# Two edits in a two-block transformer kernel: the last modulation pieces loaded ahead of the query weights, and the second block's output projection in full precision

## The chip, the cores and the metric

The kernel runs on one core of a Trainium2 chip. The metric is the device time of one execution in microseconds (us). Before the change the median of three runs is 1758.28 us (1758.21 to 1758.53).

## The reference

The input is a sequence of 256 tokens of width 1024 (two token blocks of 128) in float32. It goes through two different transformer blocks, each with two layers. What matters here, shortened:

```
# first block, per layer
shift, scale, gate, ... = split(silu(c) @ w_ada + b_ada)     # modulation, 6 x 1024 values
h = rmsnorm(x) * (1 + scale) + shift
q_lat, kv_lat, k_pe, sb_qkv, mb_qkv, gates = split(h @ w_in)
q  = rmsnorm(q_lat) @ w_uq ;  kv = rmsnorm(kv_lat) @ w_ukv   # latent attention (MLA)
merged = g_a*(o_mla @ w_o_mla) + g_b*(o_sb @ w_o_sb) + g_c*(o_mb @ w_o_moba)
x = x + gate * (merged @ w_out) ; then a squared-ReLU feed-forward

# second block, per layer
proj = rms_norm(x) @ w_in
mix = concat(o_fox, o_nsa, o_dil)                            # 256 + 512 + 256 columns
x = x + rms_norm(mix @ w_out)                                # the output projection
x = x + rms_norm(conv_ffn(rms_norm(x), w_up, conv, w_down))
```

## The kernel before

**Weights and the ring.** All weights stream from memory in pieces of at most 128 x 1024 float32 values (512 KB) through a ring of ten slots (`ring`, RAW = 10). The list `stream` is the order of the pieces, made at lines 424 to 488. SyncE issues the loads in that order (`load`, line 582): the load of piece u waits until piece u-10, which had the same slot, has been used by its reader. SyncE is one queue, so a load that waits holds all behind it. TensorE tells that a piece is free by an increment that rides on the next matmul it issues (the list `owed`); for the modulation pieces VectorE is the reader and tells it itself (`ada_used`, line 1919).

**Two kinds of product.** Most linear layers are split: a weight piece is rounded by ScalarE into a `high` part (line 1372, buffers `high` of four, or a spare place in another tensor), VectorE subtracts that from the raw piece into a `low` part (line 1813), the features are likewise held as two parts (`featT_r` and `featL`), and `three` (line 798) makes three products in the reduced format float32r: high x high, high x low, low x high. In the profile these are the matmuls on `high`, `gates_r`, `big_r` or `ring_r` with `featT_r` or `oT_r`. Other layers are plain (`plain`, `linear`, `linear_pair`): one product in full float32 from the raw piece in the ring, with no copy and no subtraction. In the profile a full-precision matmul leaves two records. `split` pieces pass through ScalarE (`highs(n)`) and VectorE (`split_unit`, `first_quarters(n)`: a unit is four pieces, a quarter is one) at places written out by hand in each engine's program.

**First block, layer 0, around the change.** The projection w_in is computed in eleven units (u = 0 to 10), then the query weights w_uq (two units of three pieces), then w_ukv (two pieces), then modulation tile 9, then the gate columns unit by unit as filling between the attention heads. The modulation product silu(c) @ w_ada is made by VectorE, piece by piece: `ada_step` (line 1906) multiplies the two halves of a piece by a scalar per partition and adds them up in `ada`, four steps for 512 columns; TensorE then sums over the partitions. The last four of these steps before MLA are done between the two copies of q out of the banks (line 2197), in layer 0 alone: in layer 1 there are none at this place (`0 if l else 4`). The gate unit's pieces stand in the stream between w_uq and those four modulation pieces. Gate unit 3 follows behind w_ukv; its copies are `highs(2 if i in (2, 3) else 0)` inside ScalarE's MLA loop (line 1599), ahead of that turn's exponentials, and its subtractions stand at the same turns on VectorE (line 2216), ahead of that turn's score subtraction.

**Second block, around the change.** The attention loop (`softmax_heads`) leaves eight chunks of 128 features x 256 tokens in an output bank each. VectorE copies six of them to `oT`; two turns later ScalarE rounds such a chunk into `featT_r` (line 1469) and VectorE takes the rest into `featL` (line 2031). The last two chunks VectorE rounds and subtracts itself, straight from the bank (lines 2039, 2040). The output projection is `two_as_ready` (line 855): tiles (token block t, column half u) in the order (0,0), (0,1), (1,0), (1,1), each over 8 chunks with `three`, and inside the last tile, after its first piece, the transposes of token block 0 for the next layer (`flip_tile`). Pieces are told free while token block 1 is computed. Behind it ScalarE squares the banks, GpSimd makes the reciprocal root (`rstd_parts`), VectorE applies it (`products`, `normed`, `scale_tokens`), the transposes follow, ScalarE and VectorE turn them into feature parts (`features_out`), and w_up starts (`two_by_tiles`, then `channels`). Between these steps the pieces of the output weights and of w_up are rounded and subtracted.

Of the kernel before, what the change touches and what calls it, by code (L numbers as in the profile page):

```python
# [8 lines left out]
F32 = mybir.dt.float32  # L9
F32R = mybir.dt.float32r  # L10
I32 = mybir.dt.int32
ACT = mybir.ActivationFunctionType
# [101 lines left out]
def two_blocks(nc, x_in, c_in, positions, w_ada, b_ada, norm1_g, norm2_g, w_in, q_norm_g, w_uq,  # L114
# [5 lines left out]
    with ctx:  # L120
# [79 lines left out]
        spare_out_2 = slots(gates_r, 0, PIECE) + slots(big_r, 6 * PIECE, 7 * PIECE)  # L200
        assert T * N_IN <= 6 * PIECE
# [81 lines left out]
        out_high, out_low = sem("out_high"), sem("out_low")  # L283
# [111 lines left out]
        def split_given(*pieces, spare=None):  # L395

            split_units.append(pieces)
            low_units.append(pieces)
            for j, it in enumerate(pieces):
                put(it, spare[j] if spare else None, False, 12)  # L400

# [22 lines left out]
        for l in range(LAYERS1):  # L424
# [8 lines left out]
            for u in range(11):  # L433
                c0 = u * ATT_W if u < 9 else ATT + 512 * (u - 9)
                split(w_in[l], (c0, min(c0 + ATT_W, ATT) if u < 9 else c0 + 512), beside=IN_STEPS[l][u - 1] if u else 0,
                      spare=spare_1 if u == 0 else None)
            for u in range(2):
                plain(*[cols_piece(w_uq[l], k0, k0 + 2, (UQ_W * u, UQ_W * u + UQ_W)) for k0 in range(0, QR // P, 2)])
            gate_unit = split(w_in[l], (ATT + 2 * 512, ATT + 3 * 512), later=True)
            for _ in range(0 if l else 4):  # L440
                ada_piece()
# [24 lines left out]
        for l in range(LAYERS2):  # L466
# [4 lines left out]
            for u in range(2):  # L471
# [6 lines left out]
                split_given(cols_piece(w, 0, 2, (cols.start, cols.stop), split=True),  # L478
                            *[piece(2, 512, [(slice(0, HD), all_k, all_n, lower[:, j:j + 2, :]),
                                             (slice(HD, P), all_k, all_n, upper[:, j:j + 2, :])], split=True) for j in (0, 2)],  # L480
                            cols_piece(w, 6, 8, (cols.start, cols.stop), split=True), spare=spare_out_2 if u else None)
# [243 lines left out]
        def _(pe):  # L725
# [514 lines left out]
            for l in range(LAYERS2):  # L1240
# [97 lines left out]
        def _(act):  # L1338
# [110 lines left out]
            def softmax_heads(jobs, beside=None, out0=None):  # L1449
                for i in range(len(jobs) + 2):  # L1450
# [14 lines left out]
                    if out0 is not None and i >= 5 and jobs[i - 5]["last"]:  # L1465
                        out0 += 1
                        act.wait_ge(outputs.read, out0)
                        c = jobs[i - 5]["chunk"]
                        act.activation(featT_r[:, c, :], oT[:, c, :], ACT.Copy).then_inc(out_high, 1)
# [181 lines left out]
            for l in range(LAYERS2):  # L1651
# [19 lines left out]
                highs(2)  # L1671
# [34 lines left out]
                softmax_heads(second_jobs, compressed, attention_out[l] - KD)  # L1706
# [878 lines left out]
```

## Time and profile before

| | |
|---|---|
| median of the runs | 1758.28 us |
| profiled execution | 1757.0 us |
| its span | 1755.3 us |
| TensorE (PE) busy | 1687.2 us, 96% |
| VectorE (DVE) busy | 1180.3 us, 67% |
| ScalarE (ACT) busy | 858.0 us, 49% |
| GpSimd (POOL) busy | 146.7 us, 8% |
| chain that ended last | TensorE 70%, VectorE 15%, ScalarE 5%, loads 4% |

The profile is of one execution. The span is the time from the first to the last recorded instruction. A line such as L1372 is a line of the kernel; a helper's line stands for all that it issues, so the matmuls all have L741 (`mm`) and the transposes L750 (`flip`), and one goes by the names of the tiles. Brackets at the end of a timeline's row give the idle time of the engine just before and what ended it. The granted clock is a share of 2.4 GHz: 1.00 is the upper level, 0.50 the lower one (1.2 GHz), values between are a mixture. `PEld` is the load of the stationary operand, which overlaps the matmuls.

### The profile page before, as it was taken

To read this page: it belongs to the slowest core of one execution; us is meant where nothing else is said; L and a number is where in the kernel's file an instruction comes from. 1 tells how busy PE (TensorE), PEld (TensorE's weight loads), DVE (VectorE), ACT (ScalarE), POOL (GpSimd) and SP (SyncE) were. 2 spreads that over 40 slices of the span, in tenths; PEclk is the share of its full clock that TensorE was granted. 3 is DMA by queue.
4 is the path that set the end of the run, shared out by engine and by line. 5 is a ranking of instruction groups with operands and counts; after the bars stand their busy time and mean duration, and the time that the engine had idled before them with its cause. 6 is when DMAs were issued, how large, how long until landed. Compare 5 with 4: busy or idle time off the path is not lost.

```text
span 1755.3 us, 24848 instructions
## 1 busy us (share of the span) xinstructions
PE 1687.2 (96%) x9315; PEld 1389.8 (79%) x9315; DVE 1180.3 (67%) x2033; ACT 858.0 (49%) x1505; POOL 146.7 (8%) x296
## 2 busy tenths in 40 slices
PE   6999799999999999999999999989999999999998
PEld 3897576589987896774799878767998787679986
DVE  5676455866766885556835675757788767667885
ACT  3354264256443442652455344475555544755552
POOL 1210011000000000220000000041000000410000
PEclk8999999999999999999999999989999999999999
DMA  9886424557863986326456656703665467046552
GB/s 341 296 280 223 149 61 141 189 192 260 291 203 122 365 272 198 116 76 217 144 204 202 193 163 201 203 2 122 214 183 187 157 219 193 1 135 210 184 181 84
DMA packets 185912, 323.71 MB, mean 184 GB/s; under 512 B 13540, under 2 KB 101184, under 8 KB 185792
## 3 DMA queue, kind: packets, MB, share of 16 engines
q1 hardware_dynamic: 183200, 320.54, 56.4%
q10 hardware_dynamic: 2592, 1.57, 0.3%
q8 instruction: 74, 1.21, 0.3%
q14 instruction: 46, 0.38, 0.1%
HBM read 321.02 MB, written 1.05 MB: 183 GB/s over the span
## 4 chain that ended last, share of the span: by engine, by line
PE 70%; DVE 15%; ACT 5%; DMA 4%; issue 3%; POOL 2%; SPq 0%; DVEq 0%; POOLq 0%; ACTq 0%
PE bank L741 67%; DVE ring_r L1813 6%; PE bank L750 3%; ACT sm L1458 1%; DMA ring<-in_w_in 1%; DVE ada L1918 1%; DMA ring<-in_w_ada 1%; POOL sm L667 1%; ACT high L1372 1%; DMA ring<-in_w_ff 1%; DVE gates_r L1838 1%; DVE sm L1998 1%; DVE gates L2496 0%; DVE oT_r L1845 0%; DVE gates L2494 0%
## 5 line engine op out<-in xcount | busy, mean ns | idle before, releaser
L1813 DVE TENSOR_TENSOR ring_r<-ring,high 128x1024 fp32r<-128x1024 f32 (+3 forms) x390 | 460.5, 1197 | 271.1 <-ACT high L1372 262.7
L1372 ACT ACTIVATE high<-ring 128x1024 fp32r<-128x1024 f32 (+3 forms) x390 | 402.1, 1037 | 482.1 <-PE bank L741 357.1
L741 PE MATMUL bank<-ring_r,featT_r 128*128 128x512 f32 (+3 forms) x928 | 355.5, 383 | 0.0
L741 PE MATMUL bank<-high,featT_r 128*128 128x512 f32 (+3 forms) x712 | 277.2, 389 | 8.9 <-DVE oT_r L1845 2.8
L741 PE MATMUL bank<-featT_r,high 128*128 128x256 f32 x960 | 272.6, 284 | 0.1
L741 PE MATMUL bank<-featT_r,ring_r 128*128 128x256 f32 x960 | 271.6, 283 | 0.0
L741 PE MATMUL bank<-oT_r,high 128*128 128x256 f32 x960 | 271.6, 283 | 0.0
L741 PE MATMUL bank<-high,oT_r 128*128 128x512 f32 (+3 forms) x712 | 270.6, 380 | 0.0
L741 PE MATMUL bank<-high,gates_r 128*128 128x512 f32 x736 | 230.2, 391 | 3.6 <-DVE ring_r L1813 2.6
L741 PEld LDWEIGHTS bank<-ring_r,featT_r 128*128 128x128 f32 x928 | 175.8, 189 | 27.2 <-issue 0.5
L741 PEld LDWEIGHTS bank<-featT_r,high 128*128 128x128 f32 x960 | 184.2, 192 | 1.2 <-DVE ring_r L1813 0.9
L741 PEld LDWEIGHTS bank<-oT_r,high 128*128 128x128 f32 x960 | 184.3, 192 | 0.3 <-issue 0.2
L741 PEld LDWEIGHTS bank<-featT_r,ring_r 128*128 128x128 f32 x960 | 184.2, 192 | 0.0
L741 PE MATMUL bank<-ring_r,gates_r 128*128 128x512 f32 x432 | 168.2, 389 | 0.0
L741 PEld LDWEIGHTS bank<-high,featT_r 128*128 128x128 f32 x712 | 133.9, 188 | 40.9 <-issue 11.8
L741 PEld LDWEIGHTS bank<-high,gates_r 128*128 128x128 f32 x736 | 138.2, 188 | 34.9 <-DVE ring_r L1813 4.6
L741 PEld LDWEIGHTS bank<-high,oT_r 128*128 128x128 f32 x712 | 133.9, 188 | 21.3
L1918 DVE SCALAR_TENSOR_TENSOR ada<-ring,tiny,ada 128x512 f32<-128x512 f32 x154 | 115.5, 750 | 12.7 <-DMA ring<-in_w_ada 7.8
L667 POOL TENSOR_TENSOR sm<-sm,rs 128x128 f32<-128x128 f32 (+1 forms) x160 | 77.2, 514 | 463.9 <-DVE rs L2021 441.0
L1458 ACT ACTIVATE sm<-sm,mx 128x128 f32<-128x128 f32 (+1 forms) x160 | 71.5, 447 | 47.5 <-DVEq L2004 47.3
L741 PEld LDWEIGHTS bank<-ring_r,gates_r 128*128 128x128 f32 x432 | 81.1, 188 | 16.3
L656 POOL TENSOR_SCALAR stat<-stat 128x1 f32<-128x1 f32 x26 | 13.3, 510 | 828.0 <-ACT sm L1390 827.9
(267 smaller groups left out, 2205.3 us busy)
## 6 DMA issues: line engine op xcount, KB each, us to landing
ring<-in_w_ff SPq DMA_DIRECT2D x128, 512.0 KB, 5.0
ring<-in_w_ada SPq DMA_DIRECT2D x96, 512.0 KB, 5.7
ring<-in_w_up SPq DMA_DIRECT2D x176, 256.0 KB, 3.4
ring<-in_w_in SPq DMA_DIRECT2D x64, 464.0 KB, 5.3
ring<-in_w_in SPq DMA_DIRECT2D x48, 512.0 KB, 5.5
ring<-in_w_in SPq DMA_DIRECT2D x48, 474.0 KB, 5.0
ring<-in_w_down SPq DMA_DIRECT2D x44, 512.0 KB, 3.5
ring<-in_w_out SPq DMA_DIRECT2D x24, 512.0 KB, 5.3
```

The costliest lines, as they stand in the source:

```text
L656: pool.tensor_scalar(stat[:, 4 + t:5 + t], stat[:, 2 * t:2 * t + 1], EPS, None, ALU.add).then_inc(pool_chain, 1)
L667: ins = pool.tensor_tensor(sm[:, n, a:z], sm[:, n, a:z], rs[:, n, t:t + 1].to_broadcast([P, z - a]), ALU.mult)
L741: ins = pe.matmul(o, a, b, start=start, stop=stop, skip_group_check=True)
L750: ins = pe.transpose(o, a, ident[0:n, 0:n])
L1372: act.activation(it["high"], it["raw"], ACT.Copy).then_inc(high_ready, 1)
L1458: ins = act.activation(sm[:, n, cols], sm[:, n, cols], ACT.Exp, scale=-1.0, bias=mx[:, n, t:t + 1], accum_out=rs[:, n, t:t + 1])
L1813: dve.tensor_tensor(it["low"], it["raw"], it["high"].bitcast(F32), ALU.subtract).then_inc(low_ready, 1)
L1838: dve.tensor_tensor(low_, src, high_.bitcast(F32), ALU.subtract).then_inc(hid_split, 1)
L1918: link(dve.scalar_tensor_tensor(out=acc, in0=row, scalar=by, in1=acc, op0=ALU.mult, op1=ALU.add))
L1998: ins = dve.tensor_tensor_reduce(out=sm[:, n, a:z], in0=b[:, a:z], in1=cst[:, j["mask"] + a:j["mask"] + z], scale=-j["scale"], scalar=3e38 ...
```

## The change

In the first block, layer 0, the four modulation pieces move ahead of the w_uq pieces in the stream (four DMAs in SyncE's queue, ahead of six of w_uq and four of the gate unit), and the four steps on VectorE move ahead of the gate unit's four subtractions, the copies of k_pe and the first copy of q. TensorE's order is the same.

In the second block, both layers, the eight pieces of the output weights become plain: no copies by ScalarE (8 per layer), no subtractions by VectorE (8 per layer). The chunks stay in `oT` in full precision; the roundings and subtractions of the chunks go, and all eight are copied from the bank once. The projection is `linear_pair`: the same order of tiles and the same transposes inside the last tile, after its first piece, with 32 full-precision products where there were 96 reduced ones. The pieces of w_up keep their places on ScalarE and VectorE relative to the steps of the norm, but for one: VectorE now has two quarters ahead of the transposes' features and none behind them, where it had three and one. The places of `high` and the count back to the piece that was there before follow from the shorter list.

```diff
-        spare_out_2 = slots(gates_r, 0, PIECE) + slots(big_r, 6 * PIECE, 7 * PIECE)
...
+            for _ in range(0 if l else 4):
+                ada_piece()
             for u in range(2):
                 plain(*[cols_piece(w_uq[l], k0, k0 + 2, (UQ_W * u, UQ_W * u + UQ_W)) for k0 in range(0, QR // P, 2)])
             gate_unit = split(w_in[l], (ATT + 2 * 512, ATT + 3 * 512), later=True)
-            for _ in range(0 if l else 4):
-                ada_piece()
             for u in range(2):
                 plain(cols_piece(w_ukv[l], 0, KVR // P, (512 * u, 512 * u + 512)))
...
-                split_given(cols_piece(w, 0, 2, (cols.start, cols.stop), split=True),
-                            *[piece(2, 512, [(slice(0, HD), all_k, all_n, lower[:, j:j + 2, :]),
-                                             (slice(HD, P), all_k, all_n, upper[:, j:j + 2, :])], split=True) for j in (0, 2)],
-                            cols_piece(w, 6, 8, (cols.start, cols.stop), split=True), spare=spare_out_2 if u else None)
+                plain(cols_piece(w, 0, 2, (cols.start, cols.stop)),
+                      *[piece(2, 512, [(slice(0, HD), all_k, all_n, lower[:, j:j + 2, :]),
+                                       (slice(HD, P), all_k, all_n, upper[:, j:j + 2, :])]) for j in (0, 2)],
+                      cols_piece(w, 6, 8, (cols.start, cols.stop)))
...
# TensorE, second block
-                seen.more(out_low, KD - 2)
                 deep_tile0.append((made[id(for_dve)], made[id(outputs)]))
-                two_as_ready({(1, 1, 1): (scaled, 0)}, (for_dve, for_dve, outputs, outputs))
+                linear_pair(lambda c, t: oT[:, c, t * P:(t + 1) * P], scaled, (1, 1))
...
# ScalarE, second block
                 turns_out(nsa_turns + fox_turns)
-                highs(2)
...
-                softmax_heads(second_jobs, compressed, attention_out[l] - KD)
-                highs(6)
+                softmax_heads(second_jobs, compressed)
+                highs(2)
                 square_banks(deep_tile0[LAYERS1 + 2 * l], (0, 0), (0, 1))
-                highs(2)
                 square_parts((0, 0), (0, 1))
...
# VectorE, attention loop: the last two chunks had been rounded and subtracted from the bank
+                        b = tile(outputs)
+                        read(outputs, dve.tensor_copy(out_view(jobs[i - 4]["chunk"], fill is not None),
+                                                      b[:, 0:S].rearrange("p (t s) -> p t s", t=T)))
...
# VectorE, first block
                 modulation_out(l, IN_OUT[l][10])
+                for _ in range(0 if l else 4):
+                    ada_step()
                 split_unit()
...
                     read(for_dve, dve.tensor_copy(qmla[:, 1, u * UQ_W:(u + 1) * UQ_W], b[:, 0:UQ_W]))
-                    for _ in range(4 if u == 0 and l == 0 else 0):
-                        ada_step()
...
# VectorE, second block
-                first_quarters(2)
                 turns_out(key_turns + dil_turns)
...
                 first_quarters(2)
-                split_unit()
                 seen.more(bc_loaded, 32)
                 products(0, 0)
                 normed(0)
                 scale_tokens([0])
-                first_quarters(3)
+                first_quarters(2)
                 features_out(pcol[:, 2 + l, 96:104], None, True, [0])
-                first_quarters(1)
                 products(0, 1)
```

## Rows read from the trace of the kernel before

**Rows 1.** The page's first part: TensorE's busy time, share, instructions.
```profile
PE 1687.2 (96%) x9315; PEld 1389.8 (79%) x9315; DVE 1180.3 (67%) x2033; ACT 858.0 (49%) x1505; POOL 146.7 (8%) x296
```
**Rows 2.** Windows: stretch, its us, TensorE busy (count), granted clock, DMA share, GB/s.
```profile
159.54:192.74 33.20, 29.01 (x93) 0.95 0.50 169
192.74:231.64 38.90, 33.54 (x197) 0.91 0.40 136
675.44:702.01 26.57, 26.17 (x85) 1.00 0.63 211
702.01:734.14 32.13, 30.87 (x197) 1.00 0.32 99
...
1184.43:1208.38 23.95, 23.20 (x104) 1.00 0.40 129
```
**Rows 3.** Windows of TensorE inside these stages, and of full-precision products (the last).
```profile
160.35:176.07 15.72, 15.72 (x50) 1.00 0.73 248
...
180.07:188.71 8.64, 8.64 (x16) 0.80 0.18 63
...
215.93:222.08 6.15, 6.15 (x22) 0.52 0.73 271
291.86:312.56 20.70, 20.70 (x48) 1.00 0.56 183
```
**Rows 4.** The chain that ended last, layer 0: start, us, what.
```profile
175.46 4.47 DMA ring<-in_w_ukv
...
204.83 5.53 DMA ring<-in_w_in
```
**Rows 5.** Timeline of SyncE's loads, layer 0 of the first block.
```profile
155.87 1.73 SPq L589 DMA_DIRECT2D ring<-in_w_uq  x2
...
175.46 6.27 SPq L589 DMA_DIRECT2D ring<-in_w_ukv  x2
...
203.47 8.75 SPq L589 DMA_DIRECT2D ring<-in_w_in  x10
```
**Rows 6.** Timeline of VectorE, the same stage.
```profile
160.92 0.16 DVE L1940 SCALAR_TENSOR_TENSOR mod<-mod,pcol 128x4 f32<-128x4 f32 x1 [0.15 <-DVE mod L1936]
...
172.64 3.22 DVE L1918 SCALAR_TENSOR_TENSOR ada<-ring,tiny,ada 128x512 f32<-128x512 f32 x4 [1.13 <-DMA ring<-in_w_ada]
```
**Rows 7.** DMA issues between 152 and 157.3: count, size, median us to landing.
```profile
ring<-in_w_uq SPq DMA_DIRECT2D x2, 384.0 KB, 3.6
```
**Rows 8.** Timeline of TensorE, projection and first w_up units, second block's layer 0.
```profile
1184.43 0.50 PE L741 MATMUL bank<-high,featT_r 128*128 128x512 f32 x1 [0.99 <-DVE oT_r L2040]
...
1185.69 0.39 PE L741 MATMUL bank<-high,oT_r 128*128 128x512 f32 x1
...
1202.04 0.39 PE L741 MATMUL bank<-gates_r,oT_r 128*128 128x512 f32 x1
1202.66 1.09 PE L750 MATMUL bank<-cst,wide 128*128 128x128 f32 x8 [0.23 <-DVE wide L1806]
...
1208.38 0.47 PE L741 MATMUL bank<-high,featT_r 128*128 128x512 f32 x1 [0.52 <-DVE oT_r L1845]
...
1221.39 0.47 PE L741 MATMUL bank<-high,featT_r 128*128 128x512 f32 x1 [0.44 <-DVE oT_r L1845]
```
**Rows 9.** VectorE, last chunk of the attention, second block's layer 1.
```profile
1532.80 0.42 DVE L2039 CAST featT_r<-bank 128x256 fp32r<-128x256 f32 x1 [1.46 <-PE bank L741]
1533.25 0.42 DVE L2040 TENSOR_TENSOR oT_r<-bank,featT_r 128x256 fp32r<-128x256 f32 x1
```
**Rows 10.** ScalarE's copies of w_up pieces, projection, second block's layer 1.
```profile
1547.89 1.06 ACT L1372 ACTIVATE high<-ring 128x1024 fp32r<-128x1024 f32 x1 [0.30 <-PE bank L741]
...
1552.63 1.06 ACT L1372 ACTIVATE high<-ring 128x1024 fp32r<-128x1024 f32 x1 [1.26 <-DMA ring<-in_w_up]
```
**Rows 11.** ScalarE at the GELU, second block's layer 0.
```profile
1127.45 0.76 ACT L1675 ACTIVATE gates<-bank 30x256 f32<-30x256 f32 x2 [2.42 <-PE bank L741]
```
**Rows 12.** The waits, whole span: us in total, times, longest.
```profile
PE bank L750 <- POOL sm L667: 12.0, 16, 5.4
```

More of the change, by code:

```diff
@@ L199, in two_blocks @@
         spare_2 = slots(gates_r, 0, PIECE) + slots(sm_r, PIECE) + slots(pT_r, 0)
-        spare_out_2 = slots(gates_r, 0, PIECE) + slots(big_r, 6 * PIECE, 7 * PIECE)
-        assert T * N_IN <= 6 * PIECE
         spare_gates = slots(oT_r, 8 * S) + slots(kvm_r, PIECE) + slots(gates_r, 5 * PIECE) + [None]
@@ L282, in two_blocks @@
         evac_act = sem("evac_act")
-        out_high, out_low = sem("out_high"), sem("out_low")
         ready_dve = sem("ready_dve")
@@ L393, in split @@
             return pieces
[L395 to L400, printed above, removed]
         def split_together():
@@ L1447, in turns_out, with softmax_heads @@
                     read(ins)
-            def softmax_heads(jobs, beside=None, out0=None):
+            def softmax_heads(jobs, beside=None):
                 for i in range(len(jobs) + 2):
@@ L1464, in softmax_heads @@
                             copy_out(pT[:, (2 * (i - 2) + e) % NPT, :], b[:, 0:3 * P])
[L1465 to L1469, printed above, removed]
             def stick_heads(l, beside):
@@ L1985, in gates_out, with out_view @@
                 read(outputs, dve.tensor_copy(n, b[:, :]))
+            def out_view(c, l1):
+                return out_of(c) if l1 else oT[:, c, :].rearrange("p (t s) -> p t s", t=T)
             def softmax_heads(jobs, beside=None, fill=None):
@@ L2027, in softmax_heads @@
                         gates_out()
-                    if fill is None and 6 <= i < len(jobs) + 3 and jobs[i - 6]["last"]:
-                        c = jobs[i - 6]["chunk"]
-                        seen.more(out_high)
-                        dve.tensor_tensor(featL[:, c, :], oT[:, c, :], featT_r[:, c, :].bitcast(F32), ALU.subtract).then_inc(out_low, 1)
                     if i >= 4 and jobs[i - 4]["last"]:
-                        b, c = tile(outputs), jobs[i - 4]["chunk"]
-                        if fill is not None:
-                            read(outputs, dve.tensor_copy(out_of(c), b[:, 0:S].rearrange("p (t s) -> p t s", t=T)))
-                        elif i < len(jobs) + 1:
-                            read(outputs, dve.tensor_copy(oT[:, c, :], b[:, 0:S]))
-                        else:
-                            link(dve.tensor_copy(featT_r[:, c, :], b[:, 0:S]))
-                            read(outputs, dve.tensor_tensor(featL[:, c, :], b[:, 0:S], featT_r[:, c, :].bitcast(F32), ALU.subtract))
+                        b = tile(outputs)
+                        read(outputs, dve.tensor_copy(out_view(jobs[i - 4]["chunk"], fill is not None),
+                                                      b[:, 0:S].rearrange("p (t s) -> p t s", t=T)))
             def stick_heads(beside, fill):
```

## The prediction

> **What bounds the kernel now.** I read the busy shares first. TensorE works for 1687.2 of 1755.3 us [rows 1], so nothing that another engine gains counts unless TensorE waits for it, and every microsecond that TensorE is given counts in full. TensorE is idle for only 68 us. The question is therefore which of its idle time the first edit takes away, and how much work the second edit adds.
>
> Next I compared the two layers of the first block over the same stages [rows 2]. They issue the same work, except that layer 0 has one more modulation tile and four more modulation pieces in the stream of loads. From the start of the query weights to the first transposes of MLA, layer 0 takes 33.20 us and layer 1 takes 26.57. From there to the next turn (the stick-breaking heads) it is 38.90 against 32.13. The granted clock is 0.95 and 0.91 in layer 0 and 1.00 in layer 1. The chain of waits names what stands in layer 0 and not in layer 1: a load of w_ukv of 4.47 us and a load of w_in of 5.53 us [rows 4]. Both have one reason, the ring of ten slots. Before the change the stream is 6 pieces of w_uq, 4 gate pieces, 4 modulation pieces, 2 of w_ukv, then the pieces of gate unit 3. So w_ukv takes the slots of the last two w_uq pieces, and unit 3 takes those of the gate pieces just ahead of it. SyncE issues w_ukv only at 175.46, the second 5.9 us later because the last w_uq piece is told free by the first matmul that itself waits for w_ukv; unit 3 is issued from 203.47 on [rows 5].
>
> **Edit 1, the four modulation pieces ahead of w_uq.** The numbers N+... count pieces from the first w_uq of before. After: modulation N to N+3, w_uq N+4 to N+9, gate N+10 to N+13, w_ukv N+14 and N+15, unit 3 N+16 to N+19. A piece waits for the one ten before it. So w_ukv waits for the first two w_uq pieces, and unit 3 for the last four. From w_uq on, these distances are those of layer 1, whose windows are thus a measured picture of what is left.
> - Stage A: 33.20 - 26.57 = 6.63, less the extra modulation tile of layer 0 (0.81 us, from 159.54 [rows 2] to w_uq's start at 160.35 [rows 3]): 5.8 us. It is made of the wait of 4.0 us between the end of w_uq (176.07) and the start of w_ukv (180.07), and of w_ukv's eight products (16 records), which take 8.64 us at a granted clock of 0.80 [rows 3], the 1.2 GHz level for a part of them after the idle time, where eight at 0.8625 (below) would take 6.9.
> - Stage B: 38.90 - 32.13 = 6.8 us. ScalarE stands in its queue at a copy that waits for unit 3's load, with the exponentials of the next head pair behind it, and TensorE waits for these through VectorE and GpSimd. Then 6.15 us run at a clock of 0.52, the lower level [rows 3].
>
> What the moved step costs. On VectorE the four steps now stand ahead of the gate unit's four subtractions and the first copy of q. Two steps take 3.22 us and the links between them [rows 6], so four take about 6.4: from 161.1 (end of the modulation sum) to 167.5. The gate loads wait for them one by one, at 162.6, 164.2, 165.9 and 167.5, where they went at 157.65 before. With 4 to 4.4 us to land, ScalarE's last copy ends at 173 and VectorE's last subtraction at 174.3, the q copies at 175.7 and 176.7. TensorE wants that unit only after w_ukv, at 183.9, so the cover is 9 us. w_ukv stands behind the gates in SyncE's queue: issued at about 168, landed at 173, wanted at 176.1. The cover is 3 us; beyond it each microsecond costs one, and then the clock. w_uq is the tight one: its first piece now takes a slot that is told free at 155.87 [rows 5], lands 3.6 us later [rows 7], at 159.5, and TensorE wants it at 160.35; the second and third have 0.6 to 1 us. I take nothing for it. Bounds of edit 1: 12.6 us at best (5.8 + 6.8), 8.9 at worst, if w_uq comes 2 us late and the clock falls for it (2 + 1.7, the latter what w_ukv lost). I take 12.6.
>
> **Edit 2, the output projection.** Before, 96 products per layer of 128x512 in the reduced format. 72 starts lie between 1185.69 and 1202.04 [rows 8]: 0.2271 us each, 21.8 us. After, 32 full-precision products of the same shape. Such a product is in the trace in the first block: 48 records, two to a product, so 24 products in 20.70 us [rows 3], 0.8625 each, 27.6 us. That is 5.8 us more per layer, 11.6 for both. It stands on TensorE and nothing hides it.
>
> The row has a full-precision product at 0.8625 / 0.2271 = 3.8 times a reduced one. The Trainium skill (FP8 and Floating Point Precision, section TensorE Precision Notes) has it as four passes through the array. By that rule, as an estimate, a product would take 4 x 0.2271 = 0.908 us and the sum would be 2.9 us longer; I go by the row.
>
> What comes back, per layer:
> - The last chunk is copied once from its bank, where before it was rounded and then subtracted, 0.42 us each [rows 9]. TensorE starts the projection 0.42 us sooner.
> - In the projection TensorE waits 0.23 us for the scaled tokens and 0.52 for their parts [rows 8]. Both tiles of token block 0 are now full 13.8 us after the start instead of 10.9, the scaled tokens follow 7.3 us behind (from 1184.43 + 10.9 to the flip's 1202.66), at 21.1, and the flip now stands at 22.4, so the 0.23 goes. The parts: w_up pieces 2 and 3 take slots that come free 16.7 and 18.4 us after the start. They land 3.8 to 4.7 us later (before: released at about 1547.9, copied at 1552.63 [rows 10]), so ScalarE copies the second from 23.1 to 24.2, squares and splits features until 26.5, VectorE, which subtracts that piece first, until about 28.2, and TensorE is done at 28.6. The 0.52 goes, with a slack of only 0.4 us.
> - VectorE has no quarter ahead of the products of token block 1 now, so that chain is 1.1 us shorter; TensorE reaches it 0.5 us sooner. The 0.44 us wait in the first w_up units [rows 8] goes: 0.4.
> Sum: 0.42 + 0.75 + 0.4 = 1.6 per layer, bounds 0.4 (only the copy) and 2.5 (the slack also takes time off other waits).
>
> ScalarE loses 16 copies of 1.06 us (as in [rows 10]) and 12 small ones, VectorE 16 subtractions of whole pieces and 16 small ones. I price them at nothing: where two copies stood before the GELU, ScalarE then waits 2.42 us for TensorE [rows 11]. At most they cut into the 12.0 us in which TensorE waits for GpSimd's rescaling [rows 12], 5.35 of which are stage B's; GpSimd is paced by itself there. Loads, their sizes and number stay.
>
> **The sum**, against the profiled execution's own 1757.0 us (span 1755.3 and 1.7 around it): -12.6 + 11.6 - 3.2 = -4.2, thus 1752.8. The median of the runs shown, 1758.28, is 1.3 us over the profiled execution, and what I predict is the median: 1754.1 us. Less than 0.2% (3.5 us) either way can't be told from no change.
>
> **Rivals.**
> 1. Unit 3 is still late: its copy needs not only the load but a free high buffer, released by the gate unit. Then only stage A is gained, -5.8 + 8.4 = +2.6: 1760.9, slower. Against it: layer 1 has the same buffers and waits 0.9 us. It decides if more than 4.2 us of stage B stay. 6%.
> 2. The full-precision products run slower in their new place. At a granted clock of 0.80 w_ukv's take 1.08 us [rows 3]; at that price 64 of them add 14 us: 1768, clearly slower. It decides from 0.93 us each. For it: the attention ahead has many short waits. Against it: the clock is 1.00 there [rows 2]. 5%.
> 3. The w_up pieces in the projection are late, the ring being held longer: 1 to 2 us of wait in each layer, 1757. The thin slack speaks for it, the relief on VectorE and ScalarE against. 13%.
> 4. w_uq late: 3.7 us are lost in edit 1, 1757.8. 8%.
> 5. A full-precision product takes four times the pitch of a reduced one here: 64 x 0.046 = 2.9 us more, 1757.0. The 24 products speak against it. 4%. (The skill's page named above would have it so.)
> 6. The relief does reach TensorE: 2 to 4 us more, 1751. GpSimd's pace speaks against. 8%.
> The forecast has 56%, its own range is 1752.5 to 1756.
>
> **How the numbers follow.** Faster by over 0.2% means under 1754.8: most of the forecast's share (48 of 56) and rival 6: 56%. Within: the rest of it and rivals 3 to 5 and most of 1 (up to 1761.8): 37%. Slower: rival 2 and a tail of 1: 7%. The range of 1750.8 to 1758.6 leaves out rivals 1 and 2 and tails.
>
> **What would show it.** In layer 0 the windows of the two stages shrink to 27.4 and 32.1 us with a clock of 1.00, and no wait of TensorE for w_ukv or of ScalarE for w_in of over 1 us is left there. w_uq's first product starts at 160.35, not later. The projection shows 64 records per layer at 0.43 us, 28.7 us from its start to w_up's instead of 23.9, with no wait of over 0.2 us at its end. The rest shifts as a block. I am wrong if layer 0 stays longer than layer 1 by more than the modulation tile, or if a full-precision product takes over 0.9 us.

## The result and the profile after

The changed kernel takes 1749.18 us (median of four runs, 1745.93 to 1749.50) against 1758.40 for the kernel before (1758.21 to 1758.82): ratio 0.9943, 95% interval 0.9926 to 0.9960, or -9.2 us by the medians where -4.2 was forecast (the ratio is one of mean times; by it the difference is -10.0). Its profiled execution took 1749.38 us (span 1747.6). The direction was right; the time lies 1.6 us below the range of 1750.8 to 1758.6. First the page's busy times after, which answer to [rows 1]:

```profile
PE 1695.3 (97%) x9251; PEld 1380.8 (79%) x9251; DVE 1156.3 (66%) x2001; ACT 838.3 (48%) x1477; POOL 142.5 (8%) x296
```

TensorE works 8.1 us more and the span is 7.7 us shorter, so its idle time fell from 68 to 52 us. Of these 16 us the forecast had accounted for about 11 (7.9 in stages A and B, by the difference of span and busy time in [rows 2], and 3.2 in edit 2).

The windows after, of TensorE alone (stretch, its us, busy time and count, granted clock, DMA share, GB/s): stages A and B of layer 0, the run of query and w_ukv products, the projection to w_up's first product, and twice the stretch from the start of the projection to the second unit of w_up.

```profile
160.24:187.61 27.37, 27.16 (x93) 1.00 0.77 262
187.61:219.53 31.92, 30.90 (x196) 1.00 0.31 100
161.05:183.58 22.53, 22.53 (x66) 1.00 0.90 307
1171.17:1199.22 28.05, 28.05 (x73) 1.00 0.33 100
1171.17:1211.51 40.34, 40.34 (x128) 1.00 0.34 105
1523.09:1563.43 40.34, 40.34 (x128) 1.00 0.33 105
```

And the last stretch before the change, which no row ahead of the prediction shows, layer 0 and layer 1 of the second block:

```profile
1184.43:1221.39 36.96, 35.71 (x161) 1.00 0.36 114
1533.73:1570.67 36.94, 35.75 (x161) 1.00 0.37 115
```

Against [rows 2], stage A went from 33.20 to 27.37 and stage B from 38.90 to 31.92, with the clock at 1.00. The query weights and w_ukv now run without a gap (22.53 us busy of 22.53). The last-named stretch, from the projection's first product to the first product of w_up's second unit, I call P from here on. It grew by 3.38 and 3.40 us. This is the number to explain: by my terms it should have grown by 5.8 - 0.75 - 0.4 = 4.65.

TensorE after, around the projection of layer 0, to compare with [rows 8] (the helper lines have moved: matmuls are now L731, transposes L740):

```profile
1171.17 22.58 PE L731 MATMUL bank<-ring,oT 128*128 128x512 f32 x52 [0.53 <-DVE oT L2016]
1193.59 1.04 PE L740 MATMUL bank<-cst,wide 128*128 128x128 f32 x8
1194.47 5.32 PE L731 MATMUL bank<-ring,oT 128*128 128x512 f32 x12
1199.22 0.80 PE L731 MATMUL bank<-high,featT_r 128*128 128x512 f32 x1
...
1207.83 1.04 PE L740 MATMUL bank<-cst,wide 128*128 128x128 f32 x8
1208.62 0.48 PE L731 MATMUL bank<-gates_r,featT_r 128*128 128x512 f32 x1
...
1211.51 0.47 PE L731 MATMUL bank<-high,featT_r 128*128 128x512 f32 x1
```

I call each group of eight transposes of scaled tokens a turn: the first is that of token block 0, the second that of block 1. The length of a turn is the time from its first transpose to the product behind it. The 52 records before the first turn are 26 products in 22.42 us, 0.862 each, as forecast. Not one wait is left in P behind its start. The second turn takes 0.79 us (1207.83 to 1208.62); before the change it took 1.13:

```profile
1216.81 1.09 PE L750 MATMUL bank<-cst,wide 128*128 128x128 f32 x8
1217.94 0.50 PE L741 MATMUL bank<-gates_r,featT_r 128*128 128x512 f32 x1
```

### The profile page after: what moved, and what is told of

The parts are those of the page before. It is cut to its first block, busy times and chain, and to the rows that moved or that the text cites. A ratio compares the mean times of both kernels' runs of the same rounds, so it can differ in the third digit from the quotient of the medians.

```text
span 1747.6 us, 24642 instructions
## 1 busy us (share of the span) xinstructions
PE 1695.3 (97%) x9251; PEld 1380.8 (79%) x9251; DVE 1156.3 (66%) x2001; ACT 838.3 (48%) x1477; POOL 142.5 (8%) x296
## 4 chain that ended last, share of the span: by engine, by line
PE 74%; DVE 14%; ACT 5%; DMA 3%; issue 2%; POOL 2%; DVEq 0%; SPq 0%; POOLq 0%; ACTq 0%
PE bank L731 71%; DVE ring_r L1795 5%; PE bank L740 3%; ACT sm L1447 2%; DMA ring<-in_w_in 1%; POOL sm L657 1%; DVE ada L1900 1%; ACT high L1361 1%; DVE gates_r L1820 1%; DVE sm L1984 1%; DMA ring<-in_w_ff 1%; DMA ring<-in_w_ada 0%; DVE gates L2470 0%; DVE gates L2468 0%; DVE gates_r L1819 0%
## 5 line engine op out<-in xcount | busy, mean ns | idle before, releaser
L1795 DVE TENSOR_TENSOR ring_r<-ring,high 128x1024 fp32r<-128x1024 f32 (+3 forms) x382 | 451.3, 1197 | 274.8 <-ACT high L1361 267.4
L1361 ACT ACTIVATE high<-ring 128x1024 fp32r<-128x1024 f32 (+3 forms) x382 | 393.5, 1037 | 484.5 <-PE bank L731 347.7
L731 PE MATMUL bank<-ring_r,featT_r 128*128 128x512 f32 (+3 forms) x864 | 330.5, 383 | 0.0
L731 PE MATMUL bank<-featT_r,high 128*128 128x256 f32 x960 | 273.0, 284 | 0.0
L731 PE MATMUL bank<-featT_r,ring_r 128*128 128x256 f32 x960 | 271.8, 283 | 0.0
L731 PE MATMUL bank<-oT_r,high 128*128 128x256 f32 x960 | 271.7, 283 | 0.0
L731 PE MATMUL bank<-high,featT_r 128*128 128x512 f32 (+3 forms) x680 | 264.7, 389 | 4.9 <-DVE ring_r L1795 2.6
L731 PE MATMUL bank<-high,oT_r 128*128 128x512 f32 (+3 forms) x680 | 257.9, 379 | 0.0
L731 PE MATMUL bank<-high,gates_r 128*128 128x512 f32 x736 | 230.1, 390 | 3.4 <-DVE ring_r L1795 2.6
L731 PEld LDWEIGHTS bank<-featT_r,high 128*128 128x128 f32 x960 | 184.3, 192 | 0.6 <-DVE ring_r L1795 0.3
L731 PEld LDWEIGHTS bank<-oT_r,high 128*128 128x128 f32 x960 | 184.4, 192 | 0.5 <-issue 0.4
L731 PEld LDWEIGHTS bank<-featT_r,ring_r 128*128 128x128 f32 x960 | 184.4, 192 | 0.0
L731 PEld LDWEIGHTS bank<-ring_r,featT_r 128*128 128x128 f32 x864 | 163.9, 190 | 25.3 <-issue 1.0
L731 PE MATMUL bank<-ring_r,gates_r 128*128 128x512 f32 x432 | 168.2, 389 | 0.0
L731 PEld LDWEIGHTS bank<-high,gates_r 128*128 128x128 f32 x736 | 138.2, 188 | 34.4 <-DVE ring_r L1795 4.3
L731 PEld LDWEIGHTS bank<-high,featT_r 128*128 128x128 f32 x680 | 127.6, 188 | 34.4 <-issue 9.2
L731 PEld LDWEIGHTS bank<-high,oT_r 128*128 128x128 f32 x680 | 127.7, 188 | 19.9
L731 PEld LDWEIGHTS bank<-ring_r,gates_r 128*128 128x128 f32 x432 | 81.2, 188 | 16.2
```

What stands on the lines that cost most here:

```text
L731: ins = pe.matmul(o, a, b, start=start, stop=stop, skip_group_check=True)
L1361: act.activation(it["high"], it["raw"], ACT.Copy).then_inc(high_ready, 1)
L1795: dve.tensor_tensor(it["low"], it["raw"], it["high"].bitcast(F32), ALU.subtract).then_inc(low_ready, 1)
```

## The experiments

All times are medians; a ratio is that to the kernel before, run on the same chip, and a difference in us stated behind a ratio is the ratio's. The whole time of one kernel scatters: the kernel before took 1753.0 to 1761.4 us over its 36 runs here. P does not: in the seven traces with the full-precision projection (five) or with extra products instead (two) it is 40.34 to 40.38, both layers.

### Edit 1 alone

The stream of layer 0 and VectorE's steps as in the changed kernel, the projection as before.

> Edit 1 alone: the four modulation pieces and their four steps are moved, the output projection stays in split form. My forecast's step for edit 1 gives -12.6 us against the kernel before, 1745.8 us, ratio 0.9928, with layer 0's two windows at 27.4 and 30 to 32 us. The trace of the changed kernel shows these windows shorter by 5.8 and 7.0 us, so the theory that edit 1 was sized right and the whole surprise lies in edit 2 gives -12.8, the same within a microsecond. The rival, that edit 2 costs its full 8.4 us and edit 1 gave the surplus, needs -17: 1741 us, ratio 0.990.

Measured: 1745.25 us, ratio 0.9930 (0.9917 to 0.9942), -12.3 us. Its windows A and B:

```profile
159.37:186.64 27.27, 27.07 (x93) 1.00 0.77 262
186.64:218.54 31.90, 30.87 (x196) 1.00 0.31 100
```

Edit 1 was sized right: 12.6 forecast, 12.3 measured. P is 36.93 and 36.96 us there, as before. The surplus is not here.

### Edit 2 alone

The changed kernel with the first block's stream and steps as in the kernel before.

> Edit 2 alone: the second block's output projection in full precision, the stream of the first block as before. My forecast's steps give 11.6 - 3.2 = +8.4 us, 1766.8, ratio 1.0048. The distances in the two traces give +2.8 us per layer (the stretch from the end of the second block's attention to the second unit of w_up), +5.6: 1764.0, ratio 1.0032. In both the 27 us of fp32 products stand in the projection at 0.86 us each; they differ only in what comes back behind it.

Measured: 1762.69 us (ten runs), ratio 1.0025 (1.0015 to 1.0035), +4.4 us. The forecast's 8.4 lies outside the interval (2.6 to 6.2). P is again 40.34, in layer 0:

```profile
1182.36:1222.70 40.34, 40.34 (x128) 1.00 0.34 105
```

By my terms it would be 36.96 + 4.65 = 41.61. The product's price is the one I had used, so the fault lies in what comes back.

### Another 4.54 us in each projection

The kernel before, with 20 more products in each projection (five at the start of each of its four banks):

```diff
-                two_as_ready({(1, 1, 1): (scaled, 0)}, (for_dve, for_dve, outputs, outputs))
+                two_as_ready({(1, 1, 1): (scaled, 0)}, (for_dve, for_dve, outputs, outputs), 5)
...
+                            for _ in range(again if c == 0 else 0):
+                                mm(b[:, 0:n], feature_parts(0, slice(t * P, t * P + P))[0], w[0][:, 0, :], True, False)
```

> The kernel before, with 20 more products in each of the second block's output projections: at the start of each of its four banks the first product is issued five times more with the same operands, each overwriting the bank, so that the result is unchanged. Everything else, all copies and subtractions of the split form too, stays. The products cost 20 x 0.2271 = 4.54 us per layer. Theory 'time': the waits behind the projection (0.23 and 0.52 us in it, 0.44 in the first w_up units, the slow turn of the scaled tokens) vanish because TensorE comes there later and the other engines catch up, whatever they have to do. Then 1.1 to 1.6 us per layer come back and the kernel is 5.9 to 6.9 us slower than before, ratio 1.0036. Theory 'relief': they vanish because ScalarE and VectorE have fewer copies and subtractions. Then nothing comes back and it is 9.1 us slower, ratio 1.0052, with the 0.44 us wait still there.

Measured: 1764.24 us, ratio 1.0037 (1.0024 to 1.0049), +6.5 us for 9.1 us of added products. P, and the second turn with the last wait:

```profile
1184.58:1224.96 40.38, 39.89 (x180) 1.00 0.34 105
1537.57:1577.93 40.36, 39.87 (x181) 1.00 0.33 105
```
```profile
1220.38 1.09 PE L750 MATMUL bank<-cst,wide 128*128 128x128 f32 x8
1221.51 0.50 PE L741 MATMUL bank<-gates_r,featT_r 128*128 128x512 f32 x1
...
1224.96 0.47 PE L741 MATMUL bank<-high,featT_r 128*128 128x512 f32 x1 [0.43 <-DVE oT_r L1847]
```

P grew by 3.42 us for 4.54, so 1.12 us per layer came back, with all copies and subtractions of the split form still there. The interval of the whole time (+4.2 to +8.6) also leaves out the 9.1 us of the theory 'relief'. That speaks for "time" as to the waits within the projection. But the wait in the first w_up units stayed at 0.43 us, and the second turn still took 1.13 us; neither theory had foreseen this split.

### The copies and subtractions put back

```diff
+            def ballast(n, width=PIECE):
+                for _ in range(n):
+                    link(act.activation(big_r[:, 0, 6 * PIECE:6 * PIECE + width], cst[:, 0:width], ACT.Copy))
...
-                softmax_heads(second_jobs, compressed)
+                softmax_heads(second_jobs, compressed, True)
+                ballast(6)
                 highs(2)
```

(and the same on VectorE with a subtraction; `True` adds a small copy or subtraction per finished chunk inside the attention loop).

> The changed kernel with the work of the split form put back on the two engines without its use: ScalarE makes eight copies of 128x1024 (two ahead of the GELU, six behind the last heads) and VectorE eight subtractions of 128x1024 (two and six at the places they had before), and both the small copies and subtractions between the heads, all on constants and into columns that nothing else uses. Theory 'time': within 0.7 us of the changed kernel, the waits stay gone. Theory 'relief': the 1.0 us per layer that TensorE saved in the first w_up units comes back, and up to 0.3 us per layer of the waits for GpSimd in the attention: 2 to 3 us slower than the changed kernel, ratio to the kernel before 0.9958 instead of 0.9943.

Measured: 1750.18 us, ratio 0.9957 (0.9943 to 0.9970). ScalarE and VectorE are busy where the split form had them so, and P does not move:

```profile
1166.77 6.49 ACT L1366 ACTIVATE big_r<-cst 128x1024 fp32r<-128x1024 f32 x6
1173.30 2.01 ACT L1361 ACTIVATE high<-ring 128x1024 fp32r<-128x1024 f32 x2
```
```profile
1168.76:1209.10 40.34, 40.34 (x128) 1.00 0.34 105
1521.00:1561.35 40.35, 40.35 (x129) 1.00 0.35 105
```

So the relief of the two engines is worth nothing in P of the changed kernel. It is worth something ahead of P. The last 31 us of each attention, from the transposes of `kvm` to the projection's first product: before in both layers, the changed kernel (30.51 in both layers), and with the work put back (31.11 and 31.12):

```profile
1153.10:1184.43 31.33, 28.43 (x211) 1.00 0.01 1
1502.14:1533.73 31.59, 28.43 (x210) 1.00 0.00 1
```
```profile
1140.66:1171.17 30.51, 28.31 (x210) 1.00 0.01 1
```
```profile
1137.65:1168.76 31.11, 28.43 (x211) 1.00 0.01 1
```

These lengths hardly scatter: 31.31 to 31.34 and 31.57 to 31.60 us in all eight traces in split form, 30.51 to 30.54 in the four of the plain full-precision form. The put-back work costs 0.6 us per layer there, 1.2 in all, and that fits the whole time, which is 1.0 to 1.6 us over the two medians of the changed kernel, with intervals that overlap.

### The changed kernel again

> The changed kernel once more, for the scatter: how much of the gap between forecast (-4.2 us) and result (-9.2) is a matter of executions. [...] If the first result was a lucky one, the ratio is now nearer to 0.9955 (-12.3 and +4.4 us of the two edits measured alone, -7.9); if the two edits help each other, it stays at 0.9943. The stretch from the start of a projection to the second unit of w_up must be 40.34 us again, to 0.05.

Measured: 1748.62 us, ratio 0.9950 (0.9936 to 0.9964), -8.8 us. P: 40.34 and 40.35. The first result was not a lucky one by much. The edits measured alone add up to -7.9, inside both intervals; whether they help each other by a microsecond can't be told.

### The modulation pieces only behind the query weights

```diff
             for u in range(2):
                 plain(*[cols_piece(w_uq[l], ...
+            for _ in range(0 if l else 4):
+                ada_piece()
             gate_unit = split(w_in[l], ..., later=True)
-            for _ in range(0 if l else 4):
-                ada_piece()
```

> Edit 1 done half: the four modulation pieces stand between the query weights and the gate unit, instead of ahead of the query weights; the steps on VectorE are where edit 1 has them; edit 2 is left out. The ring of ten then lets w_ukv wait for the last two w_uq pieces, as before, but unit 3 for the four modulation pieces, not the gate pieces. Theory 'two waits of their own': stage A stays at 33.2 us with its wait of 4 us and its lower clock, stage B falls to 30 to 32 us: -6.9 us, 1751.5, ratio 0.996. Rival 'one follows from the other' (unit 3 is late because all behind w_ukv is late, or the clock of stage B falls because of the idle time in stage A): stage B stays over 35 us, -1 us or less. Rival 'the query weights hold it': the gate pieces now wait for the first w_uq pieces, and stage A grows by 2 us or more.

Measured: 1749.12 us, ratio 0.9952 (0.9937 to 0.9967), -8.4 us. Windows A and B, and the wait for w_ukv (engine, what it waited for, us in total, times, longest):

```profile
159.45:194.10 34.65, 29.68 (x93) 0.90 0.66 223
194.10:226.04 31.94, 30.92 (x196) 1.00 0.31 100
```
```profile
PE bank L741 <- DMA ring<-in_w_ukv: 4.7, 2, 4.5
```

Stage A keeps its wait and its low clock, at 34.65 us (in three traces with the old stream it is 34.2 to 34.4, in the profiled one of before 33.2), and stage B has lost all of its excess. So stage B's wait was not a consequence of stage A's, as edit 1's two terms had them; each goes with its own distance in the ring of ten. Here stage A's idle time (4.97 us, granted clock 0.90) left stage B's clock at 1.00. The time is below the 1751.5 expected, but 1751.5 is inside the interval.

### The old order of the w_up pieces

The changed kernel, with ScalarE's first two w_up copies behind the sums of block 0 and this on VectorE:

```diff
-                first_quarters(2)
                 seen.more(bc_loaded, 32)
                 products(0, 0)
                 normed(0)
                 scale_tokens([0])
-                first_quarters(2)
+                first_quarters(3)
                 features_out(pcol[:, 2 + l, 96:104], None, True, [0])
+                first_quarters(1)
                 products(0, 1)
```

> The changed kernel with the old order of the w_up pieces on the two engines: on VectorE three of them behind the scaled tokens and one between the features and the products of token block 1 (the changed kernel has two ahead of all, two behind the scaled tokens, none there), on ScalarE the first two copies behind the sums of squares of block 0. Theory 'order': the stretch from the end of the products of token block 1 to the second unit of w_up grows from 3.68 to 4.58 us again and the wait of 0.44 us is back, as more time ahead of it (4.54 us of extra products) did not take it away and the copies and subtractions put back did not bring it back: about 0.9 us per layer, 1.8 in all, ratio to the kernel before 0.9955 or so. Rival 'later start': with the projection 4.2 us longer the order is without weight, 3.68 us stays.

Measured: 1748.68 us, ratio 0.9949 (0.9936 to 0.9962). P is 40.34 and 40.34. My theory of the order fell for this form: what the prediction gave as reason for its third returned term (no subtraction ahead of the products of block 1) has no weight here. The rival, the later arrival of TensorE, stands.

### More time, rightly placed

As the kernel with 20 extra products per projection, and four more at the start of w_up:

```diff
-                second_back = two_by_tiles(for_dve, 2)
+                second_back = two_by_tiles(for_dve, 2, 4)
```

> The kernel before with the 20 extra products in the projection and four more at the start of w_up's first bank (0.91 us), so that TensorE comes as late to the turn of block 1, seen from the start of the projection, as in the changed kernel (36.66 us; with the 20 alone 35.80). Theory 'time, rightly placed': it is this distance alone that takes the 0.9 us behind the flip away; the stretch to the second w_up unit stays at 40.4 us although 0.91 us are added, with 3.7 us instead of 4.58 behind the flip and the 0.44 us wait gone. Rival 'form': the wait belongs to the split form's copies and subtractions or their order; 4.58 us stay, 41.3 us in all. In time against the kernel before: +6.4 by the first, +8.2 by the second.

Measured: 1763.53 us, ratio 1.0034 (1.0023 to 1.0046), +6.0 us for 10.9 us of added products. P, and the second turn (the product that follows the transposes, and the second w_up unit, without a wait):

```profile
1183.39:1223.77 40.38, 40.34 (x185) 1.00 0.33 105
1537.52:1577.86 40.34, 40.29 (x184) 1.00 0.33 105
```
```profile
1219.95 1.03 PE L750 MATMUL bank<-cst,wide 128*128 128x128 f32 x8
1220.74 0.48 PE L741 MATMUL bank<-gates_r,featT_r 128*128 128x512 f32 x1
...
1223.77 0.47 PE L741 MATMUL bank<-high,featT_r 128*128 128x512 f32 x1
```

The last 0.91 us per layer cost nothing: P is the same as without them. The turn takes 0.79 us instead of 1.13 and the 0.44 us wait is gone, with the split form, its order and its engine work all untouched. So with the order of the split form it is the distance from the start of the projection to the second turn (35.80 us in the kernel with 20, 36.56 with 24, 36.66 in the changed one) that decides whether TensorE pays in the first w_up units. In the kernel before it comes 32.38 us after the start, and what releases TensorE last is VectorE's part of the features (`oT_r` in [rows 8]). With another order the distance can be shorter: in one layer of the third candidate below the turn takes 0.83 us at 31.66 us, though the wait of 0.44 us stays.

### Candidates: edit 1 with the split projection and fewer waits behind it

Three kernels on top of edit 1 alone. In the first, VectorE makes two of the w_up subtractions before it scales the tokens of block 0, and the one ahead of the products of block 1 goes behind them:

```diff
                 normed(0)
+                first_quarters(2)
                 scale_tokens([0])
-                first_quarters(3)
+                first_quarters(1)
                 features_out(pcol[:, 2 + l, 96:104], None, True, [0])
-                first_quarters(1)
                 products(0, 1)
+                first_quarters(1)
```

> A candidate that should beat both kernels: edit 1, the projection in split form as before, and on VectorE another order behind it: the first two w_up subtractions go into its idle 3.03 us ahead of the scaled tokens, one stands behind these, and the one that stood ahead of the products of token block 1 goes behind them. VectorE then turns the features of block 0 out 0.6 us sooner (the wait of 0.52 us goes) and reaches the products of block 1 sooner. Theory: the stretch from the start of the projection to the second unit of w_up falls from 36.9 us to 36.1, 1.5 us in all, 1743.8 us, ratio 0.992. Rival: ScalarE's copies of these pieces end last there, VectorE only waits elsewhere, and it stays at 36.9.

The second changes ScalarE alone:

```diff
                 square_banks(deep_tile0[LAYERS1 + 2 * l], (0, 0), (0, 1))
-                highs(2)
                 square_parts((0, 0), (0, 1))
+                highs(2)
```

> Edit 1, the projection in split form, and one move on ScalarE: in the second block the sums of squares of the new x of token block 0 stand ahead of the first two w_up copies instead of behind them. In split form these two copies wait (0.90 and 0.30 us, for TensorE) for buffers that the w_out pieces hold, and keep the squares of x, which were wanted from 1198.1, until 1199.58; in full precision they hold nothing and the copies were long made. Theory 'held buffers': the scaled tokens of block 0 come about 1.2 us sooner, the 0.23 and 0.52 us waits go, and the stretch from the start of the projection to the second unit of w_up falls from 36.96 to about 36.2 us; 1.5 us in all against edit 1 alone, 1743.8. Rival: ScalarE's order is without weight, the loads of the third and fourth w_up piece end last there, 36.96 stays.

The third adds this on VectorE to it:

```diff
                 features_out(pcol[:, 2 + l, 96:104], None, True, [0])
-                first_quarters(1)
                 products(0, 1)
                 first_quarters(1)
                 normed(1)
-                first_quarters(1)
+                first_quarters(2)
                 scale_tokens([1])
```

> As the kernel with the squares first, and on VectorE the w_up subtraction that stood between the features of block 0 and the products of block 1 goes behind these products, and the next ones each one place down (two ahead of the scaled tokens of block 1). VectorE ends its chain to the scaled tokens about 1 us sooner. Theory: beside the 0.75 us of the waits in the projection, the 0.9 us in the first w_up units (the slow turn and the 0.44 us wait) go as well: 35.2 to 35.4 us from the start of the projection to the second unit of w_up, 3.3 us in all against edit 1 alone, 1742, ratio 0.991. Rival: the subtraction only changes places within a stretch in which VectorE is busy throughout, the 4.58 us behind the flip stay and it is the same as with the squares first (36.2).

Measured: 1742.88 us, ratio 0.9916 (0.9901 to 0.9932); 1741.44, 0.9909 (0.9895 to 0.9924); 1742.27, 0.9913 (0.9899 to 0.9927). P in the second and in the third:

```profile
1168.37:1205.01 36.64, 35.55 (x160) 1.00 0.37 115
1518.98:1555.11 36.13, 35.52 (x160) 1.00 0.37 117
```
```profile
1171.63:1208.02 36.39, 35.49 (x161) 1.00 0.37 116
1520.65:1556.60 35.95, 35.18 (x161) 1.00 0.37 118
```

In the first it is 36.62 twice, 0.3 us won where 0.8 was expected: TensorE leaves 0.65 us between the two turns but pays 0.3 ahead of the first. The second wins 0.3 and 0.8 us (expected 0.75), the third 0.6 and 1.0 us (expected 1.6). In both, the wait of 0.4 us ahead of the second w_up unit stayed in both layers. These two changes of order bring at most 1 us per layer; less work on VectorE's chain was not tried. The three can't be told from each other in time and not surely from edit 1 alone (0.9930, 0.9917 to 0.9942). Their slowest run (1745.40) is still below the fastest of the nine of the changed kernel (1745.93), while those of edit 1 alone (1743.55 to 1747.23) overlap with it. What is shown to beat both given kernels is edit 1 with the split projection and one of these orders; the squares first has the lowest median.

## Why the prediction missed

- **Edit 1, right.** Stage A -5.8 forecast, -5.8 in the profiled pair; stage B -6.8 and -7.0. That it fits to 0.2 us in each stage is in part luck: the two together take 70.8 to 72.9 us in the four traces with the old stream and 59.2 to 59.5 in the eight with the new one. The clock is 1.00 in both stages after the change. w_uq's first product follows the modulation tile directly (161.05, that is 0.81 us behind 160.24, as before), so w_uq was not late. VectorE's four steps run from 161.82 to 168.15 (forecast 161.1 to 167.5, in a trace that is 0.7 us behind at that point) and w_ukv is issued at 168.65 (forecast "about 168"). The gate loads landed later than the 4 to 4.4 us that I took (median 5.3 over the loads from 150 to 230 us), so VectorE's last subtraction ended at 177.15 instead of 175.0, well inside the cover of 9 us. The timeline of SyncE's loads after, to compare with [rows 5]:

```profile
156.58 4.86 SPq L579 DMA_DIRECT2D ring<-in_w_uq  x6
163.18 5.42 SPq L579 DMA_DIRECT2D ring<-in_w_in  x4
168.65 0.98 SPq L579 DMA_DIRECT2D ring<-in_w_ukv  x2
169.81 53.55 SPq L579 DMA_DIRECT2D ring<-in_w_in  x12
```

Unit 3 is issued from 169.81 instead of 203.47. Rivals 1 and 4 are out.

- **Edit 2's price, right.** 0.862 us per product against 0.8625 taken. Rivals 2 and 5 are out. The Trainium skill (FP8 and Floating Point Precision, section TensorE Precision Notes) has true FP32 as four passes, which as an estimate gives 4 x 0.2271 = 0.908 us; the trace does not agree: 0.862 / 0.2271 = 3.80.

- **What comes back, wrong: this is the step that failed.** I had 1.6 us per layer, 3.2 in all; it was 3.5 per layer, 7.1 in all. The copy gave 0.46 (the wait ahead of the projection is 0.53 instead of 0.99 [rows 8]). P gave more, and two more places gave something that I had at nothing (next point). Before, P holds 144 products of 0.2271 us, 32.70, and two turns of 0.88 and 0.79 (their length after), 34.37 in all, and takes 36.96: 2.59 us are lost in it in layer 0. After, it holds 32 x 0.8625 + 48 x 0.2271 + 1.67 = 40.17 and takes 40.34: 0.17 are lost. So 2.42 us came back where I had 1.15. I had added up the waits that the timeline names (0.23, 0.52, 0.44: 1.19 us) and taken the rest for work. The rest was waiting too. A record is 0.39 us long where products follow each other every 0.2271, and the named idle time begins only at the record's end, so each wait is named 0.16 us too short. The products ahead of the last two waits:

```profile
1207.47 0.39 PE L741 MATMUL bank<-big_r,oT_r 128*128 128x512 f32 x1
...
1220.56 0.39 PE L741 MATMUL bank<-gates_r,oT_r 128*128 128x512 f32 x1
```

  The next starts are 1202.66 (behind 1202.04), 1208.38 and 1221.39 [rows 8]. Less one pitch each, the three waits are 0.39, 0.68 and 0.60 us, 1.68 in all. The second turn costs 0.18 ahead of it and 0.34 in it. The last 0.4 us are slower first products behind each wait. In the kernel with 20 extra products the same sum leaves 1.47 us lost, in the one with 24 0.56. So about 2.0 of the 2.4 are a matter of TensorE coming later, which the kernels with extra products show with nothing else changed. The remaining 0.4 lie between the kernel with 24 and the changed one; I have not taken them apart.

- **Outside P.** I had priced the relief of ScalarE and VectorE at nothing, with GpSimd "paced by itself". At the end of each attention it is not nothing: the stretch ahead of the projection is 0.80 and 1.07 us shorter (see the copies put back), of which 0.46 each is the single copy. The other 0.34 and 0.61 us are relief: with work put back the stretch is 0.60 us longer in each layer, which undoes it in layer 1 and rather more than undoes it in layer 0. TensorE's waits for GpSimd's rescaling there fell from 1.8 and 2.1 us to 1.6 in both layers. Without this stretch, the way from P's end to the next projection takes 280.7 to 281.1 us in either form (eight traces whose low-clock stretch in it is 10.2 us long). Behind the second P, up to the start of TensorE's last instruction, it is about 178.6 us in split form (eight traces) and 178.2 in the other (five, the one with the work put back among them). The 0.36 us stand at one place, the start of w_down in layer 1, 128 us behind P (before, then after; in layer 0 the wait is 0.39 in both):

```profile
1698.92 0.50 PE L741 MATMUL bank<-high,gates_r 128*128 128x512 f32 x1 [0.59 <-DVE gates_r L1838]
```
```profile
1691.33 0.50 PE L731 MATMUL bank<-high,gates_r 128*128 128x512 f32 x1 [0.39 <-DVE gates_r L1820]
```

  Why it shrank stays open; it is not the work taken off the engines, since it is the same with that work put back.

- **The sum of edit 2** by these: 2 x 3.39 for P, -0.8 and -1.07 ahead of it, and -0.36 behind, makes +4.5, against +4.4 measured alone and 8.4 forecast. With edit 1's 12.3 to 12.8 that gives -7.8 to -8.3. Two measurements of the whole gave -9.2 and -8.8. So some 3.9 us of the 4.9 missed are this step: 2.5 in P, 1.0 at the end of the attention (with 0.1 of the copy), 0.4 at w_down. The rest is within the intervals.

- **Rival 6**, that the relief reaches TensorE, had the number that came nearest (1751). Its reason holds for about 1 us, at the end of the attention; the larger part, in P, came without any relief, so that the number fits is in part luck. ScalarE indeed only waits longer at the GELU, 5.53 us instead of 2.42 [rows 11]:

```profile
1113.81 0.76 ACT L1658 ACTIVATE gates<-bank 30x256 f32<-30x256 f32 x2 [5.53 <-PE bank L731]
```

- **Rival 3** (late w_up pieces) did not come: TensorE goes on to w_up without a wait. How much slack that chain had I have not measured.

## What to carry to other kernels

When work is added to the engine that bounds a kernel, work out the stretch up to the point where the others have caught up as products times pitch, and take the whole difference to its measured length as what may come back, not only the waits that the timeline names: those are counted from the end of a record that is longer than the pitch, and slow turns are not among them. Other engines' chains behind a handover run from the handover: extra work there is partly free (here 2.0 of 5.45 us). For the same reason I would expect work taken away there to bring less than its length; no run here shows that. Work taken off engines that are not the bottleneck can still shorten TensorE's short waits for a chain through them (here 0.3 to 0.6 us per layer), so it is worth a look at each such wait. A load in a ring waits for what stands one ring length ahead, so moving a few pieces with another consumer between two tight ones can take out two waits at once; the second was also had alone.

## What the runs showed of the hardware

- The length of a stretch at TensorE's lower clock differs between executions of the same instructions. Two windows each of the kernel before and of edit 1 alone, which issue the same there: inside the low stretch in the second block's attention, and all from P's end to the next projection.

```profile
1488.50:1497.00 8.50, 8.49 (x33) 0.50 0.13 43
...
1221.39:1533.73 312.34, 303.86 (x1942) 0.98 0.54 166
```
```profile
1474.50:1488.00 13.50, 13.49 (x52) 0.51 0.17 56
...
1207.71:1521.98 314.27, 305.79 (x1942) 0.98 0.53 165
```

  Before, the clock's record has 10.2 us at the lower level there, with edit 1 alone 13.7. Four traces in split form with 10.2 us take 312.3 to 312.6 us for the whole stretch, four with 13.7 us 313.6 to 314.3: 1.4 us between the means. That is as large as the terms that I argued over; with a few such places in a span it may well be a good part of the scatter of one kernel's times, which I have not worked out.
- A full-precision product of 128x512 costs 0.862 us at clock 1.00 in three places of these kernels (the first block's 24 products and both projections), 3.80 times a reduced one.
